# The first piece of x in two loads, with the first unit's weights between them, and seven blocks of zeros for nine

## What is computed

```python
h = rms_norm(x, norm_mix[i])                 # x: (1, 512, 1024)
proj = (h @ w_in[i]).astype(f32)             # w_in: (1024, 3840)
qa, ka, va, qb, fb, ib, gb, qc, kc, vc = jnp.split(proj, split_at, axis=-1)
...                                          # three kinds of token mixers
x = x + mix @ w_out[i]
...                                          # gated MLP (w_up, w_down), gate with w_pg, w_pe
return rms_norm(x, norm_final)
```

## Time and profile before

| | |
|---|---|
| median of 3 runs | 732.79 us (732.59 to 733.21) |
| the profiled execution | 733.19 us, its span 731.4 us |
| PE busy | 720.6 us, 99% of the span |
| DVE, ACT, POOL busy | 62%, 43%, 16% of the span |
| DMA | 69.44 MB, mean 95 GB/s |
| granted clock, mean | 0.997 |

### The profile page before, as it was taken

How to read it: one execution, slowest core, us unless ns; L and a number is a source line. 1 busy time by engine, 2 the same in 40 slices (tenths; PEclk the granted TensorE clock), 3 DMA queues, 4 the chain that set the end, 5 groups by cost and what they waited for, 6 DMA issues and landing times.

```text
span 731.4 us, 10533 instructions
## 1 busy us (share of the span) xinstructions
PE 720.6 (99%) x3939; PEld 591.1 (81%) x3939; DVE 450.5 (62%) x733; ACT 312.8 (43%) x508; POOL 113.7 (16%) x92
## 2 busy tenths in 40 slices
PE   9999999999999999999999999999999999999995
PEld 6777778878888878888888888888888888888885
DVE  4676678587756736477676676676673333333546
ACT  5682214256666644353343343433432132225834
POOL 1012000036655522201101101101100000000000
PEclk9999999999999999999999999999999999999998
DMA  8423221312222103333323323333315323233202
GB/s 268 144 68 107 60 59 57 117 57 87 88 87 87 59 30 116 93 109 89 114 87 94 107 86 99 102 86 108 93 50 173 115 87 107 83 106 105 98 0 116
DMA packets 117425, 69.44 MB, mean 95 GB/s; under 512 B 2818, under 2 KB 112466, under 8 KB 117386
## 3 DMA queue, kind: packets, MB, share of 16 engines
q1 hardware_dynamic: 115518, 65.65, 30.2%
q10 hardware_dynamic: 1868, 3.26, 1.3%
HBM read 66.77 MB, written 2.13 MB: 94 GB/s over the span
## 4 chain that ended last, share of the span: by engine, by line
PE 96%; DVE 2%; ACT 1%; issue 1%; POOL 0%; DVEq 0%; ACTq 0%
PE bank L536 26%; PE bank L538 25%; PE bank L537 25%; PE bank L878 2%; PE bank L876 2%; PE bank L877 2%; PE bank L577 2%; PE bank L676 2%; PE bank L659 2%; PE bank L645 1%; PE bank L647 1%; PE bank L611 1%; PE bank L727 1%; PE bank L716 1%; PE bank L631 1%
## 5 line engine op out<-in xcount | busy, mean ns | idle before, releaser
L536 PE MATMUL bank<-h_hi,w_hi 128*128 128x512 f32 x582 | 232.1, 399 | 0.2 <-DVE scratch L1382 0.2
L538 PE MATMUL bank<-h_hi,w_lo 128*128 128x512 f32 x582 | 227.2, 390 | 0.0
L537 PE MATMUL bank<-h_lo,w_hi 128*128 128x512 f32 x582 | 226.9, 390 | 0.0
L948 ACT ACTIVATE w_hi<-raw 128x1024 fp32r<-128x1024 f32 (+1 forms) x104 | 108.0, 1039 | 266.5 <-PE bank L538 258.1
L1326 DVE TENSOR_TENSOR w_lo<-raw,w_hi 128x1024 fp32r<-128x1024 f32 (+1 forms) x104 | 127.2, 1223 | 88.5 <-ACT w_hi L948 88.3
L536 PEld LDWEIGHTS bank<-h_hi,w_hi 128*128 128x128 f32 x582 | 109.3, 188 | 24.0 <-issue 2.2
L538 PEld LDWEIGHTS bank<-h_hi,w_lo 128*128 128x128 f32 x582 | 109.2, 188 | 23.4
L537 PEld LDWEIGHTS bank<-h_lo,w_hi 128*128 128x128 f32 x582 | 109.4, 188 | 20.9 <-issue 0.5
L1874 POOL TENSOR_SCALAR probs<-probs,row_inv 128x512 f32<-128x512 f32 (+3 forms) x48 | 65.7, 1375 | 136.1 <-DVE row_inv L1576 136.0
L536 PE MATMUL bank<-act_hi,w_hi 128*128 128x512 f32 x176 | 68.6, 389 | 0.0
L538 PE MATMUL bank<-act_hi,w_lo 128*128 128x512 f32 x176 | 68.5, 389 | 0.0
(11 more groups left out here) (241 smaller groups left out, 943.5 us busy)
## 6 DMA issues: line engine op xcount, KB each, us to landing
raw<-in_w_up SPq DMA_DIRECT2D x44, 512.0 KB, 3.7
raw<-in_w_in SPq DMA_DIRECT2D x26, 512.0 KB, 3.8
raw<-in_w_down SPq DMA_DIRECT2D x16, 512.0 KB, 3.4
raw<-in_w_out SPq DMA_DIRECT2D x8, 512.0 KB, 3.4
raw<-in_w_pg SPq DMA_DIRECT2D x8, 512.0 KB, 3.8
bias<-bias_table ACTq DMA_DIRECT2D x6, 512.0 KB, 3.5
raw<-in_w_down SPq DMA_DIRECT2D x8, 384.0 KB, 3.0
x_rows<-in_x SPq DMA_DIRECT2D x4, 512.0 KB, 5.1
```

The source lines that it names most:

```text
L536: pe.matmul(bank, hi, x_hi, start=first, stop=False)
L537: pe.matmul(bank, hi, x_lo, start=False, stop=False)
L538: return pe.matmul(bank, lo, x_hi, start=False, stop=last)
L948: act.activation(w_hi[:, u % SPLIT, 0:nk * ncol], raw[:, u % RAW, 0:nk * ncol], ACT.Copy)\
```

## The change

The first piece of x (tiles 0 and 1) comes in two loads of 128 features each. The first keeps the semaphore x_in[0], the second has one of its own, x_second, and stands in SP's queue behind the first piece of unit 0's weights. On PE, turn_x(0) turns tile 0, runs one block of zeros and the two products of unit 0 with tile 0's high part (opening_products(0)), waits for x_second and turns tile 1. The two products with tile 1 and those with the remainders follow. keep_warm at the start has 6 blocks for 8; the block that stood behind turn_x(0) now stands inside it. ACT waits for x_second too before it squares rows of x.

```diff
@@ SP @@
+            def load_x(cols, done):
+                sp.dma_start(x_rows[:, :, cols], a["x"][0, :, cols].rearrange("(t p) c -> p t c", p=P)).then_inc(done, 16)
+
             for j in range(PAIRS_K):
                 cols = slice(2 * j * P, (2 * j + 2) * P)
-                sp.dma_start(x_rows[:, :, cols], a["x"][0, :, cols].rearrange("(t p) c -> p t c", p=P)).then_inc(x_in[j], 16)
+                load_x(slice(0, P) if j == 0 else cols, x_in[j])
                 for u in range(FIRST):
+                    if (j, u) == (0, 1):
+                        load_x(slice(P, 2 * P), x_second)
@@ PE @@
                 for k in (2 * j, 2 * j + 1):
+                    if k == 1:
+                        keep_warm(1)
+                        opening_products(0)
+                        pe.wait_ge(x_second, 16)
...
-            def opening_products():
-
-                pe.wait_ge(first_lo, 1)
-                for k in range(2):
-                    pe.wait_ge(h_hi_ready, k + 1)
-                    pe.matmul(banks[bank_of(0)][:, :], w_hi[:, 0, k * P:(k + 1) * P], h_hi[:, k, :], start=(k == 0), stop=False)
-                    pe.matmul(banks[bank_of(0)][:, :], w_lo[:, 0, k * P:(k + 1) * P], h_hi[:, k, :], start=False, stop=False)
+            def opening_products(k):
+
+                if k == 0:
+                    pe.wait_ge(first_lo, 1)
+                pe.wait_ge(h_hi_ready, k + 1)
+                pe.matmul(banks[bank_of(0)][:, :], w_hi[:, 0, k * P:(k + 1) * P], h_hi[:, k, :], start=(k == 0), stop=False)
+                pe.matmul(banks[bank_of(0)][:, :], w_lo[:, 0, k * P:(k + 1) * P], h_hi[:, k, :], start=False, stop=False)
+
+            def opening_rest():
+
                 for k in range(2):
                     wait_h(0, k)
                     pe.matmul(banks[bank_of(0)][:, :], w_hi[:, 0, k * P:(k + 1) * P], h_lo[:, k, :], start=False, stop=False)
...
-            keep_warm(8)
+            keep_warm(6)
...
             turn_x(0)
-            keep_warm(1)
             for j in range(PAIRS_K):
                 if j:
                     first_products(0, j)
                 else:
-                    opening_products()
+                    opening_products(1)
+                    opening_rest()
@@ ACT @@
                 if j == 2:
+                    act.wait_ge(x_second, 16)
```

More of the change, by code:

```diff
@@ L366, in build @@
             sem(s) for s in ("ident_in", "square_in", "masks_in", "vec_in", "conv_in", "table_in"))
-        x_in = [sem(f"x_in{j}") for j in range(PAIRS_K)]
+        x_in, x_second = [sem(f"x_in{j}") for j in range(PAIRS_K)], sem("x_second")
         piece_in = [[sem(f"piece_in{u}_{j}") for j in range(PAIRS_K)] for u in range(FIRST)]
```

## The result

| | before | after |
|---|---|---|
| median | 732.87 us | 733.74 us |
| lowest to highest of 22 | 732.30 to 733.35 | 733.18 to 736.66 |
| ratio | | 1.0022 (95% interval 1.0015 to 1.0030) |
| the profiled execution | 733.19 us, span 731.4 | 733.66 us, span 731.8 |

The changed kernel is slower: 0.9 us by the medians, 1.6 us by the ratio, which takes in every execution and not only the middle one. The two differ because its executions fall in two groups. 15 of 22 took 733.18 to 733.80 us, and 7 took 736.2 to 736.7. The kernel before has one group, 1.1 us wide.

A forecast was written before the change was run, and what follows sets the result against it. Unit 1's start on PE was taken to bound the kernel: second tile's delay of 1.39 us with no first-stage gain, less 0.80, gives +0.59; 732.79 + 0.59 = 733.4 us. Range 732.0 to 734.9, the forecast's own 733.0 to 734.2.

The forecast's parts named there:

- What bounds the kernel: Whole kernel: a prologue, then some 710 us of back-to-back PE work; unit 1's start, 9.04 us, decides the time.
- The first stage: Prologue up to the first product: 0.80 us earlier, bounds 0 and 0.86; first product at 6.55 for 7.35.
- The second tile: Tile 1's turns behind unit 0's products: gain 0 to gain 1 2.06 us for 0.58; unit 1 at 9.63.
- The clock rival: PE's clock in the prologue rises later: unit 1 +1.4 to +3.3 us, taken as +2.1, 734.9 us; chance 0.20.
- the +0.59: Start of unit 1 on PE: 9.63 us against 9.04, 0.59 us later, added to the median of 732.79.
- Helping: Prologue: tile 1 does not wait behind the first product, unit 1 starts 0.8 us earlier, 732.0 us; chance 0.10.
- a start that doesn't move: First turn on PE: PE waited for norm_mix, so the delay is 1.39 us, 734.2 us; chance 0.05.

The follow-up runs named there:

- six blocks only: Kernel before with keep_warm(6) for keep_warm(8) at the start, nothing else; median 732.68 us, ratio 1.0001.
- The order alone: Kernel before with only the PE order changed (tile 0, two products, tile 1, two products), one x load, eight zero blocks; median 734.17 us against 733.03, ratio 1.0015.
- the late profile: Profiled execution of the changed kernel timed again with nothing edited; 736.27 us, span 734.4; that series had a median of 733.67 us.
- eight blocks back: Changed kernel with keep_warm(8) for keep_warm(6) at the start again; median 734.16 us.
- the second hole filled: Changed kernel with three zero blocks added behind tile 1's turns, the hole ahead of the first product left as it is; median 733.66 us.
- the loads alone: Kernel before with only x's first piece split into two loads, unit 0's weights between them; median 732.84 us against 733.03, ratio 0.9998.

## Why the prediction held, and where it was off

**What bounds the kernel** was right. Whatever moves unit 1's start moves the end by the same: 9.04 and a span of 731.4, 9.46 and 731.8, 8.57 and 730.8 with six blocks only (0.47 of start, 0.6 of span). Some 700 us of work behind it gave nothing back. It added something only where the clock was still low in unit 1: with unit 1 at 11.20 for 9.04 the span was 3.0 longer and not 2.2.

**The first stage** was to gain 0.80, between 0 and 0.86, with norm_mix unknown. It gained 0.86: PE turned norm_mix at 4.31, right behind the sixth block. Here the load did not bind; with x in one load it did (4.68). The half of x landed at 3.54, earlier than my 3.95. At the first gain the stage is 0.93 earlier (5.59 for 6.52), 0.07 beyond my bound: the clock rose during these turns, so that from first turn to gain it was 1.08 for 1.15.

**The second tile** was the step that carried the sign. I had 2.06 us from gain 0 to gain 1; it was 7.60 - 5.59 = 2.01. From gain 1 to unit 1 I had 1.85; it was 9.46 - 7.60 = 1.86. Unit 1 was forecast for 9.63 and came at 9.46. Of that difference of 0.17, 0.13 is the first stage (gain 0 at 5.59 for 5.72). The order alone, timed by itself, cost 1.1 us by the medians where the same terms give 1.39; its only profile was of a late execution, so which term is smaller in the others is not shown.

**The clock rival** had the right mechanism, and the late profile the right numbers: unit 1 at 11.20 for a forecast of 11.11, and with unit 1's own products a total between my +2.1 and +3.3 (span 734.4 for 731.4, +3.0). What I had wrong was its form. I gave it a chance of 0.20 as one way in which the kernel as a whole could go. It is a share of the executions, about one in three, beside the ordinary ones, so the measured time is a mixture: a median of +0.87 with the forecast's mechanism, and a ratio drawn up by the third that is late. What was mis-sized is thus the +0.59 as a shift of the median, and it lies below the interval of the ratio (1.1 to 2.2 us). Profile against profile the shift is 0.42, less than my sum; ordinary executions are 0.7 to 0.9 above the median of before, more than my sum. So 733.4 came as near to 733.74 as it did in part by luck. The step that my sum lacks is this: I set the shift of one profiled execution on the median of a kernel whose executions spread over 1.1 us, and as the experiment with eight blocks shows, part of that spread is the time at which the clock rises. In an execution where it rises early, taking blocks away gains less than 0.43 each, while the wait for the gain costs the same. Two profiles with an early rise bear this out, eight blocks back (above) and the second hole filled (six blocks at the start, its three extra ones behind tile 1's turns; 733.26 us):

```profile
4.32 0.22 PE L772 MATMUL bank<-square,vec_rows 8*128 8x8 f32 x1
...
9.03 0.50 PE L541 MATMUL bank<-h_hi,w_hi 128*128 128x512 f32 x1
```

Two blocks fewer bring the turn of norm_mix from 4.83 to 4.32 and unit 1 from 9.55 to 9.03, so they are worth 0.51 there and not 0.86, and in both the gains stay 2.01 apart. For such an execution my estimate is 0.88, the 1.39 that the order costs in my sum less 0.51, and from the fastest of before to the fastest of the changed kernel it is 733.18 - 732.30 = 0.88. That this is the whole of the spread is argued, not shown: no fastest execution of before was profiled.

**The page of the Trainium skill** that I weighed, "TensorE: Matmul & The Clock Gate", says in Part 1 that the stretch over which the clock gate watches TensorE runs freely and does not start anew with a kernel, so that one kernel warms up at different points from run to run. The profiles agree: of the same program, the block at 5.28 took 0.50 us in one profile, at the full pace, and 0.78 in the late one, where the full pace came only at 13.3. On its rule that transposes do not count as activity (Part 4) the runs don't decide. With zero blocks in either hole no execution was late, but no kernel here put something else in place of the transposes.

**Helping** and **a start that doesn't move** did not happen; the first product moved by 0.93, and unit 1 went the other way.

## What to carry to other kernels

On this kernel the order on one engine made "work on each piece as it lands" a chain: the turn of the second tile stood behind products that waited for another engine's work on the first, and that round trip (2.0 us) replaced a step of 0.58 in which the two engines overlapped. Count the round trips between engines ahead of the dense part, not the time at which the first product starts. Where a start-up holds filler that keeps the clock's rise on time, look at a dozen or more executions: holes of 0.4 to 0.8 us on PE hardly showed in the median, but as a second group 2.9 us later, and with one more zero block of 0.43 us in the first of them none of 11 executions was late and the median stayed (733.63).

## What the runs showed of the hardware

TensorE's pace at the start differs between executions of one program: the same chain of turns and products ran at 0.23 us a product in one profile and at 0.43 up to 12.9 us in another, 2.6 us of span apart. The granted clock in the rows of the profile stands at 1.00 in both. The group of late executions made up 11 of 34 with six blocks at the start and holes behind them, 2 of 22 with eight blocks and the holes, 0 of 33 with six and at least one hole filled, and 0 of 11 with six blocks in the old order, without these holes. The chips were not the same in all of these.

The 512 KB of x at the head of SP's queue landed 4.0 us after issue in the kernel before, the 256 KB of its first half 2.8 us in the changed one (3.2 with the loads alone), and norm_mix, 4 KB on the other queue, 3.3 us after issue beside the 512 KB (six blocks only).
